# Ninth chunk of the experts' weights in four transfers, each let go by a quarter of the first chunk

## What is computed

```python
def expert_ffn(xb, w1, b1, w2, b2):
    h = xb @ w1 + b1                       # w1: 1024 x 2048
    gate, up = h[:, :D_FF], h[:, D_FF:]
    gate = jnp.minimum(gate, SWIGLU_LIMIT)
    up = jnp.clip(up, -SWIGLU_LIMIT, SWIGLU_LIMIT)
    glu = gate * jax.nn.sigmoid(SWIGLU_ALPHA * gate)
    return ((up + 1.0) * glu) @ w2 + b2    # w2: 1024 x 1024
```

## Time and profile before

| | us |
|---|---|
| median of 3 runs | 1426.85 |
| lowest and highest run | 1426.83, 1428.99 |
| profiled execution, its own time | 1426.69 |
| its span | 1425.1 |
| TensorE busy (matmuls) | 1353.2 |
| VectorE, ScalarE, GpSimd busy | 387.4, 252.3, 94.2 |

### The profile page before, as it was taken

How to read it: one execution, slowest core, us unless ns; L and a number is a source line. 1 busy time by engine, 2 the same in 40 slices (tenths; PEclk the granted TensorE clock), 3 DMA queues, 4 the chain that set the end, 5 groups by cost and what they waited for, 6 DMA issues and landing times.

```text
span 1425.1 us, 17289 instructions
## 1 busy us (share of the span) xinstructions
PE 1353.2 (95%) x7193; PEld 704.2 (49%) x7193; DVE 387.4 (27%) x711; ACT 252.3 (18%) x375; POOL 94.2 (7%) x163
## 2 busy tenths in 40 slices
PE   8999999999999999999989989889899898998997
PEld 6667668788887543443333334333333333332342
DVE  4235443642501331221221212212121122111223
ACT  1233343321000431111111101111011111101112
POOL 1122212210000210000000000000000000000000
PEclk9999999999999999999999999999999999999999
DMA  9987879874433589999999999999999999999997
GB/s 349 373 317 276 306 250 344 284 269 156 154 127 155 222 376 428 434 429 430 433 431 432 431 431 432 431 431 433 430 431 433 431 430 434 430 430 435 423 428 293
DMA packets 43298, 519.94 MB, mean 365 GB/s; under 512 B 5194, under 2 KB 5754, under 8 KB 21460
## 3 DMA queue, kind: packets, MB, share of 16 engines
q1 hardware_dynamic: 29136, 471.67, 79.1%
q0 software_dynamic: 12576, 44.62, 9.1%
q10 hardware_dynamic: 1540, 2.99, 0.5%
HBM read 497.63 MB, written 21.67 MB: 364 GB/s over the span
## 4 chain that ended last, share of the span: by engine, by line
PE 71%; DMA 26%; DVE 1%; SPq 1%; issue 0%; ACT 0%; DVEq 0%; ACTq 0%
PE bank L1846 24%; PE bank L1533 23%; DMA arena<-in_w_pairs 15%; DMA ring<-in_w_pairs 12%; PE bank L1811 4%; PE bank L1581 4%; PE bank L1797 3%; PE bank L1898 2%; PE bank L1676 2%; PE bank L1550 1%; SPq L632 1%; PE bank L1642 1%; PE bank L1844 1%; PE bank L1807 1%; PE bank L1875 1%; PE bank L1863 1%
## 5 line engine op out<-in xcount | busy, mean ns | idle before, releaser
L1846 PE MATMUL bank<-ring,arena 128*64 128x512 f32 x1536 | 348.4, 606 | 34.7 <-DMA ring<-in_w_pairs 34.7
L1533 PE MATMUL bank<-arena,ring 128*128 128x264 f32 x1472 | 335.7, 388 | 0.0
L1533 PEld LDWEIGHTS bank<-arena,ring 128*128 128x128 f32 x1472 | 277.5, 190 | 52.0 <-issue 6.0
L1846 PEld LDWEIGHTS bank<-ring,arena 128*64 128x64 f32 x1536 | 112.5, 139 | 247.7 <-issue 229.2
L1898 PE MATMUL bank<-ring,arena 128*64 128x512 f32 x768 | 172.6, 595 | 3.1 <-DMA ring<-in_w_pairs 3.0
L1846 PE MATMUL bank<-arena 128*64 128x512 f32 x512 | 118.4, 610 | 13.2 <-DMA arena<-in_w_pairs 13.2
L1898 PEld LDWEIGHTS bank<-ring,arena 128*64 128x64 f32 x768 | 55.1, 137 | 101.4 <-issue 99.6
L1463 DVE TENSOR_SCALAR arena<-bank 128x512 f32<-128x512 f32 x32 | 22.1, 691 | 272.5 <-PE bank L1846 272.5
L1846 PEld LDWEIGHTS bank<-arena 128*64 128x64 f32 x512 | 37.0, 140 | 87.8 <-issue 87.8
L1482 DVE COPY arena<-bank 64x512 f32<-64x512 f32 x32 | 21.9, 683 | 181.4 <-PE bank L1898 181.4
L1453 DVE TENSOR_TENSOR hs<-hs,bank 128x256 f32<-128x256 f32 x16 | 6.7, 421 | 225.3 <-PE bank L1807 225.3
(11 more groups left out here) (241 smaller groups left out, 995.5 us busy)
## 6 DMA issues: line engine op xcount, KB each, us to landing
ring<-in_w_pairs SPq DMA_DIRECT2D x59, 4096.0 KB, 28.9
arena<-in_w_pairs SPq DMA_DIRECT2D x19, 4096.0 KB, 27.1
ring<-in_w_mixer SPq DMA_DIRECT2D x58, 1024.0 KB, 8.6
ring<-in_w_pairs SPq DMA_DIRECT2D x26, 2048.0 KB, 12.7
arena<-in_state_ret POOLq DMA_DIRECT2D x32, 512.0 KB, 7.4
out_ret_sample<-arena POOLq DMA_DIRECT2D x32, 512.0 KB, 6.2
arena<-in_w_pairs SPq DMA_DIRECT2D x8, 2048.0 KB, 16.2
arena<-v_decode POOLq DMA_DIRECT2D x32, 256.0 KB, 6.9
```

The lines of the kernel that those rows point to most:

```text
L1533: ins = pe.matmul(bank[:, 0:T], weight(n + k // 4, k % 4)[:, 128 * j:128 * (j + 1)], rhs[:, k, :], start=k == 0, stop=k == KD * groups - 1)
L1846: ins = pe.matmul(out, xgT[:, k, 64 * e:64 * (e + 1)], held(n, 2 * D * (k % W1_KS) + c), start=False, stop=k == KD - 1)
```

## The change

Chunk 8 of the first pair goes in four transfers of 0.5 MB in place of one of 2 MB, each of 4 KB for each partition. Transfers one to three each wait until the matmuls of their quarter of chunk 0 are done, for which three matmuls of the first `first_layer` increment a new semaphore `part_used`; the fourth waits for the whole chunk, as the single transfer did. The first three increment `early_in`, a semaphore that the mixer's weights used before, the fourth increments the place's. TensorE waits for both ahead of chunk 8. In the branch for further rounds the first pair's chunk 8 is cut in four as well, and waits as before.

```diff
@@ -462,6 +462,7 @@
         chunk_used = sem("chunk_used")
+        part_used, early_in, early_base = sem("part_used"), chunk[1], MIXER_CHUNKS // RING
@@ -631,6 +632,16 @@
                                 .then_inc(mine_in[f] if f < W2_FS - 1 else slot_in[at], 16)
+                    elif (first or alone and half == 0) and n == WIDE_SLOTS:
+                        if not first:
+                            is_free(n)
+                        for f in range(W2_FS):
+                            if first and f < W2_FS - 1:
+                                sp.wait_ge(part_used, f + 1)
+                            elif first:
+                                is_free(n)
+                            sp.dma_start(dst[:, D * f:D * (f + 1)], mine[:, D * f:D * (f + 1)])\
+                                .then_inc(early_in if f < W2_FS - 1 else slot_in[at], 16)
                     elif first or alone or last:
                         is_free(n)
                         sp.dma_start(dst, mine).then_inc(slot_in[at], 16)
@@ -1819,6 +1830,8 @@
                     at = slot_of(half, n)
+                    if first and n == WIDE_SLOTS:
+                        pe.wait_ge(early_in, 16 * (W2_FS - 1) * (r + 1) + 16 * early_base)
@@ -1837,6 +1850,8 @@
                         for q in range(2):
+                            if first and e == 0 and 0 < 2 * k + q < 2 * W1_KS:
+                                ins.then_inc(part_used, 1)
                             for side in range(2):
```

## The result

The change makes the kernel slower by a little: 1430.86 us median of 20 runs (1427.46 to 1432.58) against 1428.38 of 20 runs of the kernel before (1426.81 to 1429.65), ratio 1.0016, 95% interval 1.0009 to 1.0023, so +2.3 us. The prediction was 0.6 us less and a range up to 1428.0, so it missed in sign and in size. With 20 runs the kernel before stands 1.5 us above the median of three on which the sum was based; the rest of the miss is the change.

The account below looks back on a forecast made before the run. The prediction took the unbroken stream of the experts' weights by DMA as the bound. Of 2.6 us at the head 0.6 get through: 1426.69 less 0.6 is 1426.1, plus 0.16 for the median, forecast 1426.2 us, range 1425.0 to 1428.0.

Parts of the forecast that it names:

- the idle stretch in front of chunk 8: Weights' queue without DMA at 508 to 510 us, because chunk 8 is issued only at 509.65, when chunk 0 is used.
- the releases until 540 us: Times at which TensorE gives places free; claimed fixed whatever the stream does, since TensorE runs at its own pace up to 668.
- cost of the signals: Three increments on TensorE's existing matmuls: claimed nothing; upper bound 1.3 us later release at 539.0, a loss of 0.7.
- pieces of 4 KB rows: Chunk 8's quarters on the wire: 411 GB/s against 430, 5.1 us for the chunk, 0.2 more, claimed hidden.
- the head start: Chunk 8's first quarter issued 2.6 us earlier, landing 2.4 earlier; the whole 2.4 reaching the end was a rival at 0.07.
- the term of 0.6 us: Part of the 2.6 us at the head claimed to reach the stream behind 547 us and the end; 0.1 to 1.1.
- the transfer issued at 539.0: Second pair's third chunk, waiting for chunk 6; took 8.5 us, claimed only 0.6 above the floor, so the queue runs dry.
- the floor: Least time from issue to landing of a 2 MB transfer into an empty queue, 7.9 us: 4.9 movement, some 3.0 latency.
- the second pair's first chunk, issued at 528.3: Issued when chunk 4 is used, took 9.4 us, 1.5 above the floor; claimed to pass 1.5 us of gain.
- nothing or a loss up to 1 us: Rival at 0.18: no gain (1426.85) because the floor at 539.0 is 8.4 or new chunks upset the queue, or up to 1 us lost.
- The two rivals for "slower": Chunk 8's pieces: fixed part paid in series, 1433.5, chance 0.03; SyncE stuck in the four issues, up to 1447.9, chance 0.03.
- a cost in series: Skill rule on chunk 8: 2.0 us fixed per transfer, 12.8 us in place of 6.8, estimated 6.0 more; prediction held it overlaps.

Follow-up runs that it names:

- signals_only: Kernel before, chunk 8 still one 2 MB transfer, plus the three TensorE increments and SyncE's three waits for them; ratio 1.0002 (0.9993 to 1.0011).
- quarters_two: Kernel before with only the first pair's chunks 8 and 9 in quarters, each let go by its quarter; ratio 1.0012 (1.0003 to 1.0021).
- quarters_four: Kernel before with the first pair's chunks 8, 9 and the second pair's 0, 2 in quarters, each let go by its quarter; ratio 0.9998, and 0.9998 again when repeated.
- pieces_late: Changed kernel without head start: chunk 8's four pieces all let go only when the whole first chunk is used; ratio 1.0005 against the kernel before, median 1429.96 us.
- later_1: Kernel before, chunk 8 in one transfer let go one quarter of chunk 1 later (0.86 us); ratio 1.0014 (1.0005 to 1.0023).
- code_shifted: Kernel before with 96 additional semaphore increments at the head of TensorE's program; ratio 1.0072 (1.0058 to 1.0086).

## Why the prediction was wrong

**What held.** The bound is the stream of weights; the idle stretch in front of chunk 8 is real; the releases until 540 us are TensorE's own and didn't move (signals_only); no cost of the signals can be seen; pieces of 4 KB rows cost 0.2 us a chunk; in the first profile chunk 8 lands 2.4 us earlier (mean 8.34 for 10.76) and chunk 9 1.5 (14.17 for 15.65). That the head start is lost where a transfer of the second pair is let go late is the mechanism of the forecast, and quarters_two against quarters_four shows it. The 2.4 and 1.5 were in part luck: in the second profile they are 1.5 and 0.8.

**What failed is the term of 0.6 us**, the part of the head start said to get past the transfer issued at 539.0 ("only 0.6 us above the floor"). It measured a *loss* of 0.7: mean 40.94 and 40.92 against 40.25. Three things are in it.

- *Most went one release earlier.* The prediction let 1.5 us pass at the second pair's first chunk, issued at 528.3. At chunk 11 the mean was still 1.49 and 0.82 us ahead in the two profiles, at this one 0.45 and 0.02 (29.98 and 30.41 for 30.43). It had 30.43 - 22.31 = 8.12 us from issue to mean landing in before, 1.0 above the 7.12 of an empty queue (next point), not 1.5.
- *At the transfer of 539.0 the time in hand was 0.13, not 0.6.* I took the landings of the earlier trace rows, which are those of the last of 16 engines, 0.8 us behind the mean for chunk 8 and 1.3 at the second pair's chunk 2. In the mean chunk 8 landed 10.76 - 3.64 = 7.12 us after its issue into an empty queue, and the transfer of 539.0 took 40.25 - 33.00 = 7.25. What the 8.5 in the earlier trace rows had over 7.9 was, but for 0.13, a late engine and not time spent behind others.
- *The floor isn't a constant.* I let a landing be the later of "issue plus 7.9" and "the one before plus 4.9". Into the empty queue, the mean came 7.12 us after the issue for chunk 8 of before, and within 0.1 of that in the five other profiles in which it goes in one transfer. It was 7.09 for chunk 9 of after (14.17 - 7.08), but 7.66 and 7.93 for the second pair's chunks 0 and 2 of after (29.98 - 22.32, 40.94 - 33.01). In its second profile all three were longer, 7.75, 8.09 and 7.91. So a restart at the second pair's chunks cost 0.5 to 1.0 more than the 7.12 at the head, in both profiles; why is open. A head start that runs into such a place isn't used up but turned round: it makes a dry moment where before there was just none. The rival of "nothing or a loss up to 1 us", at 0.18, had a higher floor at 539.0 among its reasons (8.4 for 7.9) and is the nearest in kind; but it ended at 1 us of loss, and 2.3 came.

**What wasn't in the prediction at all** is the last engine. From the second pair's chunk 3 to the last piece the mean's loss stays at 0.6 to 0.8 us, but TensorE waits for the last engine, and this one was 4.10 and 2.45 us behind the mean at the end, for 1.9 in before: another 2.2 and 0.6. The part that repeats is there behind the restarts: at the second pair's chunk 3 the last engine is 2.07 and 2.11 behind the mean in the two profiles, 1.29 and 1.20 in those of before, so 0.8 more, and 2.13 in quarters_two, which has the same two restarts. But pieces_late and later_1, with no head start, have 1.83 and 1.70, so the restarts aren't shown to be its only source. It isn't made up: in all 14 profiles the lag is larger at the last piece than at this chunk. The rest came between there and the end and differs from profile to profile (2.0 and 0.3 in after, 0.6 and 0.75 in before). 0.7 us of mean and 1.4 of lag (the mean of the two profiles) are the 2.1 that stand against a measured 2.3; how near the two come is partly chance, since the two profiles have 2.2 and 0.6 of lag.

The two rivals for "slower" were not it: each piece took 4.0 to 5.5 us to landing (4.0 to 6.7 in the second profile) and they landed 1.3 to 1.9 us after one another, so no fixed part of 3 us was paid in series; the four issues took 0.33 us each, the longest of the second profile 0.73. With the first goes what the Trainium skill would have said as a cost in series ("DMA: Bandwidth & Descriptors", the rule of the section "Bandwidth" with the fixed 2.0 us of "Anatomy of one DMA", which that section fits to transfers issued from GpSimd; these are SyncE's). It gives slower, but by an estimated 6 us and in chunk 8, where the measured kernel was 2.4 and 1.5 us faster.

**What stays open.** Why a restart in the middle of the stream costs more than one at its head, and why the head start itself was anything from 1.0 to 2.4 us.

For the lag that differs by 1.7 us between two profiles of one kernel a cause fits. Some packets of 16 KB carry instructions, 34 in each profile (35 in code_shifted):

```profile
q8 instruction: 34, 0.56, 0.2%
```

In after one of 1.10 us starts at 578.4, and from the transfer before it to the one behind it the distance between first and last engine grows by 1.3; the same happens around the one at 1347.9.

```
after: landing of the last engine, distance to the first
574.80  2.93
580.96  4.19
605.65  4.50
...
1324.42 4.53
1343.84 4.53
1354.80 5.77
```

From 719 to 1330 us there is no such packet, and the distance stays within 0.02 us of 4.53. Before has as many of them: there the distance goes from 2.50 to 3.24 around the one at 713.8. Behind the second pair's chunk 3 the 14 profiles have 34 steps from one landing to the next in which the last engine falls back by more than 0.15 us against the mean. Each of the 34 has an instruction packet between the two landings or less than 3 us before the first. All profiles have 12 such packets there, and most of them add nothing. That goes well with a packet which keeps one engine for 0.9 to 1.1 us and tells only if it is an engine that is late already; which engine has it the trace doesn't show, and no run took the packets away. So it is argued, not shown. code_shifted, which moves them to other points of the program, ended with the lag of before. later_1's additional 0.3 us isn't explained.

## What to carry to other kernels

An idle stretch of the bounding queue is worth only what the *next* releases can pass on. Walk the chain to the end, and count time in hand there in units that leave out the lag of single engines; where it was 0.1 and 1.0 us here, starting earlier bought a dry moment, which cost more than it gave. If the stretch is to be filled, fill the short places behind it at the same time (quarters_four took the loss of 1.0016 back to 0.9998), and expect little more than that: here pieces moved at 411 in place of 430 GB/s, and none of the kernels in quarters or halves was shown to be faster than the kernel before.

Compare two profiles from a common event, here the start of the first layer: it varied by 1.2 us between two profiles of one kernel, twice the effect that was forecast.

## What the runs showed of the hardware

- A packet of 16 KB occupied its DMA engine for 0.61 us in a full queue, and the first ones behind the dry moments of after for up to 1.5; the rate stayed at 336 to 344 GB/s for 4 us behind the one at 541, though the queue held work again.
- A transfer of 2 MB landed, by the mean of the 16 engines, 7.0 to 7.2 us after its issue into the empty queue at the head of the stream (six profiles), and 7.7 to 8.1 behind the dry moments at the second pair's chunks 0 and 2 (two profiles of after).
- The 16 engines of one stream were apart by 3.5 us from first to last on the last piece before (both profiles), by 6.0 and 4.4 in after, and by 1.1 at chunk 8 of before. Only the last one counts for the waiting engine. While no instruction packet came, from 719 to 1330 us, the distance didn't move.
- 96 semaphore increments at the head of TensorE's program moved its first matmul from 6.86 to 16.06 us. Three increments on matmuls that stand there already moved nothing (64 records in 13.90 us with and without).
